# The first modulation of an input block on TensorE, in pairs of shift and scale

## What is computed

```python
def rmsnorm(x, g):
    xf = x.astype(jnp.float32)
    y = xf * lax.rsqrt(jnp.mean(xf * xf, axis=-1, keepdims=True) + EPS)
    return y.astype(x.dtype) * g

def modulate(h, shift, scale):
    return h * (1.0 + scale) + shift
...
        mod_lat = (jax.nn.silu(c) @ w_mod[l] + b_mod[l])[:, None, :]
        mod_ctx = jax.nn.silu(c_ctx) @ w_mod[l] + b_mod[l]
        sh1, sc1, g1, sh2, sc2, g2 = jnp.split(mod_lat, 6, axis=-1)
        sh1c, sc1c, g1c, sh2c, sc2c, g2c = jnp.split(mod_ctx, 6, axis=-1)
        p_lat = modulate(rmsnorm(x, norm1_g[l]), sh1, sc1) @ w_in[l]
        p_ctx = modulate(rmsnorm(ctx, norm1_g[l]), sh1c, sc1c) @ w_in[l]
```

## Time and profile before

| | us |
|---|---|
| three runs, median (lowest to highest) | 2462.7 (2458.34 to 2462.7) |
| the profiled execution | 2457.67 |
| its span, first to last instruction | 2455.9 |
| mean granted TensorE clock in it | 0.967 of full |
| PE busy in the span | 2298.3 (94%) |
| DVE busy | 1348.0 (55%) |
| ACT busy | 971.0 (40%) |

### The profile page before, as it was taken

The page is one execution under the profiler, slowest core; times in us unless marked ns, Lnnn a source line. Parts: engine busy times, 40 slices in busy tenths (PEclk is TensorE's granted clock), DMA queues, the critical chain, the costliest instruction groups (busy, mean ns, idle before and its releaser), DMA issues.

```text
span 2455.9 us, 31012 instructions
## 1 busy us (share of the span) xinstructions
PE 2298.3 (94%) x12406; PEld 1834.7 (75%) x12406; DVE 1348.0 (55%) x2090; ACT 971.0 (40%) x1585; POOL 173.3 (7%) x132
## 2 busy tenths in 40 slices
PE   3899899999999989999998999999999899999997
PEld 2788787765787768888876568888888657888885
DVE  8566687786686345433455644444454564434445
ACT  3445465433425532332454544222234364322222
POOL 0000000001200100000133010000011302000002
PEclk8989999985999999999999999999999999999998
DMA  6223424641455222322231112232223202222222
GB/s 248 103 95 120 178 97 154 194 132 43 139 152 189 76 81 95 100 97 95 96 101 55 41 44 94 95 100 97 94 95 102 68 2 70 97 99 95 95 100 80
DMA packets 117616, 252.27 MB, mean 103 GB/s; under 512 B 45088, under 2 KB 49952, under 8 KB 116704
## 3 DMA queue, kind: packets, MB, share of 16 engines
q1 hardware_dynamic: 108320, 234.02, 28.7%
q10 hardware_dynamic: 9152, 16.26, 2.0%
HBM read 225.07 MB, written 25.17 MB: 102 GB/s over the span
## 4 chain that ended last, share of the span: by engine, by line
PE 79%; DVE 8%; ACT 5%; DMA 3%; issue 3%; SPq 1%; POOL 0%; ACTq 0%; DVEq 0%
PE bank L1351 19%; PE bank L1353 18%; PE bank L1352 18%; PE bank L989 4%; PE bank L1232 2%; DVE cacc L2170 2%; DMA raw<-in_s_qkvx 1%; PE bank L1513 1%; PE bank L1502 1%; PE bank L988 1%; DMA modw<-in_w_mod 1%; PE bank L1084 1%; PE bank L1086 1%; PE bank L1085 1%; PE bank L1220 1%
## 5 line engine op out<-in xcount | busy, mean ns | idle before, releaser
L1823 ACT ACTIVATE whi<-raw 128x1024 fp32r<-128x1024 f32 (+1 forms) x268 | 278.7, 1041 | 925.2 <-PE bank L1353 917.9
L1351 PE MATMUL bank<-ahi,whi 128*128 128x512 f32 x1152 | 453.4, 394 | 9.8 <-DVE alo L2607 6.9
L1352 PE MATMUL bank<-alo,whi 128*128 128x512 f32 x1152 | 449.5, 390 | 0.0
L1353 PE MATMUL bank<-ahi,wlo 128*128 128x512 f32 x1152 | 449.2, 390 | 0.0
L2493 DVE TENSOR_TENSOR wlo<-raw,whi 128x1024 fp32r<-128x1024 f32 (+1 forms) x268 | 327.5, 1222 | 139.5 <-ACT whi L1823 139.1
L1351 PE MATMUL bank<-bhi,whi 128*128 128x512 f32 x736 | 286.6, 389 | 0.0
L1353 PE MATMUL bank<-bhi,wlo 128*128 128x512 f32 x736 | 286.3, 389 | 0.0
L1352 PE MATMUL bank<-blo,whi 128*128 128x512 f32 x736 | 286.3, 389 | 0.0
L1351 PEld LDWEIGHTS bank<-ahi,whi 128*128 128x128 f32 x1152 | 217.2, 189 | 60.7 <-issue 11.3
L1352 PEld LDWEIGHTS bank<-alo,whi 128*128 128x128 f32 x1152 | 217.1, 188 | 45.7 <-issue 1.4
L1353 PEld LDWEIGHTS bank<-ahi,wlo 128*128 128x128 f32 x1152 | 217.0, 188 | 45.4
(11 more groups left out here) (433 smaller groups left out, 3684.4 us busy)
## 6 DMA issues: line engine op xcount, KB each, us to landing
raw<-in_s_gu SPq DMA_DIRECT2D x88, 512.0 KB, 3.3
raw<-in_s_qkvx SPq DMA_DIRECT2D x34, 512.0 KB, 4.6
late_modw<-in_w_mod SPq DMA_DIRECT2D x32, 512.0 KB, 3.8
raw<-in_s_up SPq DMA_DIRECT2D x32, 512.0 KB, 3.3
raw<-in_s_down SPq DMA_DIRECT2D x32, 512.0 KB, 3.2
raw<-in_s_dn SPq DMA_DIRECT2D x32, 512.0 KB, 3.3
raw<-in_s_win SPq DMA_DIRECT2D x24, 512.0 KB, 3.3
raw<-in_s_zg SPq DMA_DIRECT2D x16, 512.0 KB, 3.7
```

The lines of the kernel that those rows point to most:

```text
L1351: pe.matmul(out, w_hi, x_hi, start=start, stop=False)
L1352: pe.matmul(out, w_hi, x_lo, start=False, stop=False)
L1353: return pe.matmul(out, w_lo, x_hi, start=False, stop=stop)
L1823: act.activation(whi[u % 2][:, 0:width[u + 2] * P], raw[u % 2][:, 0:width[u + 2] * P], ACT.Identity).then_inc(hi_ready, 1)
```

## The change

Shift and scale of the first modulation are computed on PE. The pieces of `w_mod` for them are laid out as weights (`w_mod0`, sixteen units of 128 x 1024), and the two vectors as columns (`c_cols`, 128 x 16, so two columns for each block of 128 input features). For block b, a pair of pieces (b for the shift, 8+b for the scale) is multiplied: 16 matmuls of a 128 x 128 f32 weight with a moving operand of two columns (`mod_columns`). DVE no longer has the 32 multiplications; it adds the bias and forms the gain for each block ahead of its scaling (`first_modulation`). `xt` is issued ahead of all pieces. The row of c for the later sums is loaded and put through silu later; GpSimd's clearing of `cbuf` waits for the last pair.

```diff
-            for gr in range(3):
-                early_mods(gr)
             sp_.dma_start(cf[:, :], a["cf"]).then_inc(const_loaded, 16)
             sp_.dma_start(xt[:, :], a["xt"]).then_inc(x_loaded, 16)
-            early_mods(3)
+
+            def mod_pair(b):
+
+                for m in (b, KB + b):
+                    sp_.dma_start(modw[m][:, :], a["w_mod0"][m]).then_inc(pair_loaded[b], 16)
+
+            mod_pair(0)
...
                         if j == 1:
+                            for b in range(1, KB):
+                                mod_pair(b)
+                            sp_.wait_ge(mod_full, 1)
+                            sp_.dma_start(c_rows[:, :], a["c_rows"]).then_inc(c_loaded, 16)
...
+            def mod_columns(b):
+
+                if b == 0:
+                    pe.wait_ge(c_ready, 1)
+                pe.wait_ge(pair_loaded[b], 32)
+                for m in (b, KB + b):
+                    for s in range(KB):
+                        mm = pe.matmul(bank[6 + b % 2][:, 2 * m:2 * m + 2], modw[m][:, s * P:(s + 1) * P], c_cols[:, 2 * s:2 * s + 2],
+                                       start=s == 0, stop=s == KB - 1)
+                mm.then_inc(mod_full, 1)
+
+            mod_columns(0)
+            mod_columns(1)
             for s in range(KB):
                 pe.wait_ge(lo_out, 2 * (s + 1))
                 for u in range(2):
                     mm = block_products(u, s)
                     if s == KB - 1:
                         mm.then_inc(unit_done, 1)
+                if s + 2 < KB:
+                    mod_columns(s + 2)
...
-            for v in range(2):
-                act.activation(c_rows[:, v * D:(v + 1) * D], c_rows[:, v * D:(v + 1) * D], ACT.Silu).then_inc(c_ready, 1)
+            act.activation(c_cols[:, :], c_cols[:, :], ACT.Silu).then_inc(c_ready, 1)
...
+            act.wait_ge(c_loaded, 32)
+            act.activation(c_rows[:, :], c_rows[:, :], ACT.Silu).then_inc(c_ready, 1)
             need(small_loaded, 32)
             act.activation(wsmhi[:, :], wsm[:, :], ACT.Identity).then_inc(small_by_act, 1)
...
+            def first_modulation(b):
+
+                dve.wait_ge(mod_full, b + 1)
+                after(dve.tensor_tensor(mv[:, 0:2, b], bank[6 + b % 2][:, 0:32].rearrange("p (c b m) -> p c b m", c=2, m=2)[:, :, b],
+                                        vc("b_mod", 0, 16).rearrange("p (c b) -> p c b", c=2)[:, :, b:b + 1].broadcast_to((P, 2, 2)), ALU.add))
+                after(dve.scalar_tensor_tensor(out=aff[:, 0:16].rearrange("p (n b) -> p n b", n=2)[:, :, b], in0=mv[:, 1, b], scalar=1.0,
+                                               in1=ex(vc("norm1", b, 1), 2), op0=ALU.add, op1=ALU.mult))
...
             for b in range(KB + 1):
                 if b < KB:
+                    first_modulation(b)
...
-            pool.wait_ge(scaled, 1)
+            pool.wait_ge(mod_full, KB)
```

More of the change, by code:

```diff
@@ L135, in layout @@
     a["w_small"] = np.ascontiguousarray(w_in[:, small].reshape(KB, P, 64).transpose(1, 0, 2).reshape(P, KB * 64))
-    a["w_mod"] = np.ascontiguousarray(np.asarray(w_mod)[0].T.reshape(48, P, D))
-    a["c_rows"] = np.ascontiguousarray(np.broadcast_to(np.concatenate([np.asarray(c)[0], np.asarray(c_ctx)]), (P, 2 * D)))
+    a["w_mod0"] = units(np.asarray(w_mod)[0], r(2048))
+    a["w_mod"] = np.ascontiguousarray(np.asarray(w_mod)[0].T.reshape(48, P, D)[16:])
+    a["c_cols"] = np.ascontiguousarray(np.stack([col(np.asarray(c)[0]), col(c_ctx)], 2).reshape(P, 2 * KB))
+    a["c_rows"] = np.ascontiguousarray(np.broadcast_to(np.asarray(c)[0], (P, D)))
     wo = np.asarray(w_out)[0]
@@ L316, in build_kernel @@
         tmp = [at(f"tmp{s}", 136 + 3 * s, (P, TOK)) for s in range(2)]
-        modw = at("modw", 36, (P, 16 * D))
-        junk = [at(f"junk{s}", 164 + 4 * s, (P, D)) for s in range(3)]
+        MODKB = (188, 84, 142, 150, 164, 172, 180, 196), (192, 88, 146, 154, 168, 176, 184, 203)
+        modw = [at(f"modw{n}{b}", kb, (P, D)) for n, kbs in enumerate(MODKB) for b, kb in enumerate(kbs)]
+        c_cols = at("c_cols", 35.28125, (P, 2 * KB))
         macc = at("macc", 33.625, (P, 96))
-        c_rows = at("c_rows", 188, (P, 2 * D))
+        c_rows = at("c_rows", 188, (P, D))
         smf = at("smf", 180, (64, TOK))
@@ L364, in late_mods @@
             return range(16 + (u - 2) * 3 // 2, min(48, 16 + (u - 1) * 3 // 2)) if 2 <= u < 24 else ()
[L366 to L370 removed]
         def late_loaded(m):
[L374 removed]
+            return 32 + 16 * ((m - 16) // 4 + 1)
         def rows(t, off=0):
@@ L700, in stream @@
                                 sp_.wait_ge(mod_summed, m - 19)
-                            sp_.dma_start(late_modw[m % 4][:, :], a["w_mod"][m]).then_inc(mod_loaded[m % 4], 16)
+                            sp_.dma_start(late_modw[m % 4][:, :], a["w_mod"][m - 16]).then_inc(mod_loaded[m % 4], 16)
                         if j == 22:
@@ L2095, in after @@
                 dve.wait_ge(dve_done, marked[0])
[L2097 to L2108, removed]
             need(const_loaded, 32)
@@ L2117, in late_sum @@
                                          op0=ALU.mult, op1=ALU.mult, accum_out=macc[:, 2 * m:2 * m + 1]).then_inc(mod_summed, 1)
[L2119 to L2132, removed]
-                    after(dve.scalar_tensor_tensor(out=aff[:, 8 * n:8 * n + 8], in0=src, scalar=1.0, in1=vc(gain), op0=ALU.add, op1=ALU.mult))
-                if lo:
-                    for n, c in enumerate((2, 3, 5)):
-                        after(dve.tensor_copy(aff[:, 24 + 8 * n:32 + 8 * n], mv[:, c, :, 0]))
@@ new lines, in _ @@
+            mv = modv[:, :].rearrange("p (c b m) -> p c b m", c=6, m=2)
+            def first_modulation(b):
[4 more added lines that the diff above has]
+                                               in1=ex(vc("norm1", b, 1), 2), op0=ALU.add, op1=ALU.mult))
@@ new lines, in late_modulation @@
+            def late_modulation():
+                dve.wait_ge(mod_summed, 32)
+                after(dve.tensor_tensor(mv[:, 2:6, :, 0], macc[:, 32:96].rearrange("p (c b m) -> p c b m", c=4, m=2)[:, :, :, 0],
+                                        vc("b_mod", 16, 32).rearrange("p (c b) -> p c b", c=4), ALU.add))
+                after(dve.scalar_tensor_tensor(out=aff[:, 16:24], in0=mv[:, 4, :, 0], scalar=1.0, in1=vc("norm2"), op0=ALU.add, op1=ALU.mult))
+                for n, c in enumerate((2, 3, 5)):
+                    after(dve.tensor_copy(aff[:, 24 + 8 * n:32 + 8 * n], mv[:, c, :, 0]))
```

20 lines of the change are left out of this document (10 added, 10 removed).

## The result

| | before | changed |
|---|---|---|
| median of the runs (lowest to highest), us | 2461.12 (2458.34 to 2462.7, 4 runs) | 2501.47 (2495.38 to 2510.49, 4 runs) |
| the profiled execution, us | 2457.67 | 2507.5 |
| its span, us | 2455.9 | 2505.7 |
| mean granted TensorE clock | 0.967 | 0.953 |

The ratio is 1.0168, 95% interval 1.0149 to 1.0187: 40 us slower. The profiled execution of the changed kernel lies 6 us above its median, and the executions differ by 15 us; where that comes from is taken up with the experiments.

The account below looks back on a forecast made before the run. Two start chains, DVE's multiplications and the input's, were taken to end together near 47.5 us. First product 41.3, six turns 67.2 and last blocks 6.0 gave 114.5 against 73.5, 41 later: 2501 us, range 2475 to 2521.

Parts of the forecast that it names:

- the ring: In the block loop, products, pair, small DVE instructions, scaling and hlo run in turn: 8.27 us at full clock, 13.46 at half.
- the price of a pair: On PE, a pair's 16 matmuls make 32 passes and take 3.43 us at full clock, 6.86 at half, with nothing hidden.
- The stage: From the start to the last product of units 0 and 1: 73.5 us before, 114.5 forecast, 41 us later.
- x first: At the start, 6.8 MB less ahead of xt: it lands at 13.0 us instead of 29.2, moving the squares' chain by 16.2.
- Two chains ending together: At the start, DVE's multiplications and the input's chain both end near 47.5 us, so removing one alone gives nothing.
- Pairs 0 and 1: Ahead of the loop on PE from 27.3 us: pair 1 done at 38.6, first product at 41.3, the clock falling partway.
- The mixture of clocks: In the loop, the clock rises in four turns of six, each saving 3.4 us: 67.2 us for six turns; chance 0.60.
- half clock throughout: Rival: the whole loop at half clock, the stage ending at 132.2 us, total 2516.4 (2521 from the median); chance 0.17.
- Nothing given back behind the stage: After units 0 and 1, both kernels run nearly the same instructions, so the 41 us delay stays to the end.
- Full clock: Rival: the whole loop at full clock, units 0 and 1 ending at 91.7 us, 18 later, total 2475.9; chance 0.13.
- Cheap pairs: Rival: on PE, weights load behind the matmul ahead, so pairs cost near zero; not slower, 2455 to 2462 us; chance 0.04.
- even free pairs gain only 2.4 us: At full clock with pairs costing nothing, a turn of 4.84 us a block gives back the start's gain: total 2455.3 us.

Follow-up runs that it names:

- input-first experiment: The kernel before with only the constants and the input issued ahead of all of w_mod: 2470.0 us, ratio 1.0029.
- the version with wide products in the waits: The changed kernel with twelve 128x512 products, results unused, added on PE behind each pair of the loop: 2489.6 us, ratio 1.0111.
- the spread pairs: The changed kernel with the 16 matmuls of pair s+2 placed one or two behind each of the twelve products of block s: 2514.6 us, ratio 1.023.
- twice-issued: The changed kernel with each pair's 16 matmuls issued twice, the second time over the first: 2566.7 us, ratio 1.0408.
- the thin pairs: The changed kernel with only one of the eight matmuls for each piece of w_mod, same order: 2472.4 us, ratio 1.0039.
- all pairs ahead: The changed kernel with all eight pairs on PE ahead of block 0 instead of between blocks: 2489.1 us, ratio 1.012.

## Why the prediction was right

2501 us was predicted and 2501.5 measured. The direction, the ring and the price of a pair were right; the agreement to half a microsecond is luck. The stage was 11.6 us longer than the sum, and a second series of the same kernel gave 2514.9, also inside the range of 2475 to 2521. Step by step:

- **x first.** Worked out: `xt` at 13.0, sums at 27.3, split of unit 1 at 33.7. Measured: 14.2, 28.6, 34.9. The term was 1.2 us too good: the moved bytes were counted at 419 GB/s, while the transfers left ahead of `xt`'s end ran at 393 from 6 to 8 us and 383 from 10 to 14. Why they were slower was not tried.
- **Two chains ending together.** Half of it is borne out by the input-first experiment: DVE's chain sets the start once the input is early. The other half is a reading of rows.
- **A pair's price** from one-column rows: 3.43 and 6.86 us. Measured 3.63 (in the version with wide products in the waits; 3.49 from the start of the pair to the start of what follows) and 6.82.
- **Pairs 0 and 1** done at 38.6, first product at 41.3: measured 39.6 and 42.3, about what `xt` was late.
- **The ring.** A turn at half clock 13.46: measured 13.52. This is the term that carries the result, and it is within half a percent; its parts are 4.00 of products (3.84 worked out), 6.82 of pair (6.86) and 2.69 of DVE and signals (2.76), so small errors cancel.
- **The mixture of clocks** is the step that was mis-sized. I took a rise in four turns of six, each worth 3.4 us; the profiles show one of six and none of six, worth 3.0. The six turns took 78.1 us, not 67.2, and the stage ended at 126.1, not 114.5, nearer to the case of half clock throughout (132.2). That products had run for at least 3.4 us ahead of each rise in the rows was read as reaching the 3.84 of a turn; it should have weighed more that two of the three had taken 5.2 and 5.4. But the length of the products did not decide it here: the one rise came about 2.9 us into the products of its turn (82.84 to about 85.8), and five turns with 4.0 us of products had none. What decided it stays open.
- **Nothing given back behind the stage.** True to unit 33 (52.7 us), then not quite: 2.8 us less at the end in one execution, 6 more in the other. "The delay at the end is not the delay at that point" was one of the prediction's own signs of being wrong, and in size this step is: from the first unit's copy to the end of the span the delay changed in every profile, by -2.8 (the first of the changed kernel) to +8.3 us (the spread pairs: 57.2 to 65.5), and by +4.1 with the input first, alone (6.3 to 10.4). The 2.8 us given back and a median 6 us below the profiled execution are what brought the number back to 2501. How many rises the two executions of 2495.4 us had in the loop is not known, since no profile of them was kept.
- **The rivals.** Half clock throughout was nearest to the profiles. Full clock is out. Cheap pairs are out: by the twice-issued and the spread pairs a pass keeps its price wherever it stands. The floor of 25 ns between small matmuls that the Trainium skill names ("TensorE: Matmul & The Clock Gate", Back-to-back issue gap) does not describe these, each of which loads new f32 weights: the least seen here was 109 ns a pass (3.49 us for 32) with two columns and 107 with one. Its statement that a load goes by the columns of the weights (same page, LDWEIGHTS) fits: in the kernel before, a load of 128x64 weights took 134 ns and one of 128x128 189 at full clock, and it made no difference whether 256 or 512 columns were moved against them.
- **The worked statement that even free pairs gain only 2.4 us** was for full clock and was not tried as such. The nearest run is that of the thin pairs: at an eighth of the work, and a mixed clock, the kernel was still 9 us slower than before.

## What to carry to other kernels

Before work is moved to an engine that the loop already waits for, draw the waits of one turn: a step that stood outside the loop can close a ring, and the order in which the helping engine takes the old and the new block decides whether it does. Matmuls with one or two moving columns and new weights for each took 107 to 113 ns a pass at full clock, not the time of their columns, and a TensorE that ran little else did so mostly at half clock, with waits (0.53) and without (0.56), which doubled the price here. An idle gap of an engine is the place for such work, in the amount that fits: two pairs of eight, with an earlier input, gained 0.4% where eight cost 1.7%.

## What was unexpected of the hardware

- Adding 72 wide products of no use made the kernel 12 to 25 us faster: the clock then stood at full in the pairs (3.63 us for 6.82).
- Two series of the same program differed by 13 us in the median (2501.5 and 2514.9), while the medians of the kernel before stayed within 3.2 us (2461.1, 2459.8, 2463.0, 2461.8) and the four executions with all pairs ahead within 1.4. The spread comes with the change, but 9 of the 12 us between the two profiled executions arose in stages that it doesn't touch, a part of them at a wait for a transfer.
- PE ran thin matmuls for 49.7 us without a wait, and the granted clock still averaged 0.56.
